# A decoder layer with 64 experts: a shorter choice of experts, and a part of the shared expert's products moved into the first pair

## The reference

```python
scores = sigmoid(h @ router_w)                   # 256 tokens x 64 experts
sel = scores + router_bias
group_score = sum of the two highest sel in each of 8 groups of 8 experts
emask = experts of the 4 best groups             # ties: the lower index
eidx = top 6 of where(emask, sel, -inf)
w = scores[eidx] / sum(scores[eidx]) * 2.5
routed = sum over the chosen experts of w * ((silu(h @ w1) * (h @ w3)) @ w2)
shared = (silu(h @ sw1) * (h @ sw3)) @ sw2       # one expert that sees all tokens
x = x + gate_f * (routed + shared);  out = rms_norm(x)
```

## Time and profile before

| | us |
|---|---|
| median of 3 runs | 773.07 (772.6 to 773.08) |
| the profiled execution | 774.05 |
| its span, first to last instruction | 772.3 |
| PE busy | 734.6 (95%) |
| DVE busy | 327.5 (42%) |
| ACT busy | 173.5 (22%) |
| DMA, mean over the span | 352 GB/s |

### The profile page before, as it was taken

How to read it: one execution, slowest core, us unless ns; L and a number is a source line. 1 busy time by engine, 2 the same in 40 slices (tenths; PEclk the granted TensorE clock), 3 DMA queues, 4 the chain that set the end, 5 groups by cost and what they waited for, 6 DMA issues and landing times.

```text
span 772.3 us, 12450 instructions
## 1 busy us (share of the span) xinstructions
PE 734.6 (95%) x5030; PEld 384.8 (50%) x5030; DVE 327.5 (42%) x812; ACT 173.5 (22%) x348; POOL 8.1 (1%) x21
## 2 busy tenths in 40 slices
PE   4899999999999999999999999999999998899995
PEld 1478888888887444334343333334334342333332
DVE  1107694764456576333334333231333332322334
ACT  3213330200000232212222222221212222212223
POOL 0200001000000000000000000000000000000000
PEclk9999999999999999999999999999999999999998
DMA  9999635886969578999999999999999999999991
GB/s 338 380 349 364 211 107 196 267 263 228 293 200 408 242 304 306 369 423 421 418 380 418 421 420 420 415 421 415 421 421 422 416 417 421 421 421 419 421 393 71
DMA packets 76165, 271.46 MB, mean 352 GB/s; under 512 B 4728, under 2 KB 33536, under 8 KB 53456
## 3 DMA queue, kind: packets, MB, share of 16 engines
q1 hardware_dynamic: 74544, 264.78, 87.8%
q0 software_dynamic: 1264, 5.79, 2.0%
q10 hardware_dynamic: 304, 0.13, 0.1%
HBM read 269.62 MB, written 1.05 MB: 350 GB/s over the span
## 4 chain that ended last, share of the span: by engine, by line
PE 73%; DMA 19%; SPq 3%; DVE 2%; ACT 1%; issue 1%; DVEq 0%; ACTq 0%
PE bank L1145 71%; DMA ring<-exp_w_dram 16%; DMA ring<-w_in_dram 3%; SPq L369 2%; PE bank L1516 1%; SPq L372 1%; DMA reg<-reg 1%; DVE h_hT L1136 0%; DVE bank L1099 0%; DVE reg L982 0%; PE bank L1234 0%; ACT L618 0%; ACT h_hT L643 0%; ACT reg L530 0%; DVE y_part L1103 0%
## 5 line engine op out<-in xcount | busy, mean ns | idle before, releaser
L1145 PE MATMUL bank<-ring,h_hT 128*32 128x512 f32 (+2 forms) x2112 | 262.4, 589 | 11.5 <-DMA ring<-exp_w_dram 11.5
L1145 PE MATMUL bank<-h_hT,ring 128*128 128x256 f32 x704 | 155.9, 380 | 2.5 <-DMA ring<-w_in_dram 2.5
L1145 PEld LDWEIGHTS bank<-ring,h_hT 128*32 128x32 f32 (+1 forms) x2112 | 80.6, 114 | 153.3 <-issue 133.3
L1145 PEld LDWEIGHTS bank<-h_hT,ring 128*128 128x128 f32 x704 | 133.2, 190 | 22.2 <-ACT h_hT L502 2.1
L1145 PE MATMUL bank<-ring,const_misc 128*32 128x512 f32 x1008 | 116.5, 595 | 0.7
L1099 DVE TENSOR_TENSOR bank<-bank,reg 128x512 f32<-128x512 f32 x64 | 44.5, 695 | 54.6 <-PE bank L1145 54.6
L1103 DVE TENSOR_TENSOR y_part<-bank,y_part 128x512 fp32r<-128x512 f32 x64 | 44.2, 691 | 42.5 <-ACT y_part L669 21.2
L1145 PEld LDWEIGHTS bank<-ring,const_misc 128*32 128x32 f32 x1008 | 30.2, 109 | 62.3 <-issue 57.6
L658 ACT ACTIVATE reg<-bank 128x256 f32<-128x256 f32 x32 | 12.3, 386 | 205.3 <-PE bank L1145 205.3
L1082 DVE TENSOR_TENSOR reg<-reg,bank 128x256 f32<-128x256 f32 x32 | 13.5, 421 | 102.2 <-ACT reg L658 102.2
L1145 PEld LDWEIGHTS bank<-take,h_part 128*128 128x128 f32 x288 | 38.8, 190 | 28.6 <-issue 27.6
(11 more groups left out here) (234 smaller groups left out, 459.1 us busy)
## 6 DMA issues: line engine op xcount, KB each, us to landing
ring<-exp_w_dram SPq DMA_DIRECT2D x171, 1024.0 KB, 14.8
ring<-ada_w_dram SPq DMA_DIRECT2D x24, 1024.0 KB, 12.7
ring<-w_in_dram SPq DMA_DIRECT2D x24, 1024.0 KB, 12.2
ring<-exp_w_dram SPq DMA_DIRECT2D x35, 512.0 KB, 13.5
ring<-w_branch_dram SPq DMA_DIRECT2D x4, 1024.0 KB, 12.8
ring<-w_out_dram SPq DMA_DIRECT2D x4, 1024.0 KB, 8.9
ring<-shared_w_dram SPq DMA_DIRECT2D x2, 1024.0 KB, 15.2
spare<-exp_w_dram SPq DMA_DIRECT2D x2, 1024.0 KB, 14.5
```

What stands on the lines that cost most here:

```text
L1145: return pe.matmul(o, lhsT, rhs, start=start, stop=stop, skip_group_check=True)
```

## The change

In `pick`, the count of the greater ones comes from the comparison itself (`accum_out`), the running count of the equal ones starts from it instead of zero, and the limit is the constant k; the comparisons take the k-th value as a scalar column. The add of the two marks is left to the caller: for the groups it goes into one step with the making of the mask, and the mask is multiplied by 1e30 where it is added to `sel`. In `place`, `iota` counts from 1, so that `pos` needs no subtraction, and the four comparisons are one of 256 columns. Both leave what is chosen as it was.

Of block 1's shared products, the steps k = 5, 6 and 7 (`SHARED_CUT`) move from before the gathers into the first pair, ahead of its first gather. Since the gathered tokens overwrite hT, ACT first copies these three slices to `hT_late`; DVE and PE wait for it (`hT_kept`). Block 1 uses bank 2 instead of 4. ACT's second shared sigmoid and DVE's `shared_product(1)` move into the first pair too, and one step of the others, k = 2, moves behind `rank(1)`. `cast_out(7)` moves ahead of DVE's first copy and uses bank 3, which the second first gather writes, so that this gather waits for it. The two first w2 transfers of half 1 are asked for behind the upper halves of pair 2's w1/w3, since `sh_done` comes later. The first body of ACT and DVE is written out instead of a loop.

```diff
             def load_pair(r, use, it, halves, first_e=0):
...
                     for e in range(first_e, 2):
                         for w in range(first_e if cols == HIGH else 0, 2):
                             load_13(r, e, w, it, cols)
+                if isinstance(use, int) and use == 1 and r == 0:
+                    first_load_2(1)
                 sp.wait_ge(w2_used[r], use)
...
             shared_sigmoid(0)
-            shared_sigmoid(1)
+            act.activation(hT_late[:, :, :], hT[:, SHARED_CUT:KD, P:2 * P], ACT.Copy).then_inc(S["hT_kept"], 1)
...
                     act.activation(give[:, r, :], bank[B_Y[0]][:, 0:P], ACT.Copy)\
                        .then_inc(S["give_read"], 1)
+                    if isinstance(use, int) and n == 0:
+                        shared_sigmoid(1)
                     copy_gathered(0)
...
                 link(dve.max(top8[:, tb, :], vals))
-                kth = top8[:, tb, k - 1:k].to_broadcast([P, n])
-                link(dve.tensor_tensor(m_gt, vals, kth, ALU.is_gt))
-                link(dve.tensor_tensor(m_eq, vals, kth, ALU.is_equal))
-                link(dve.tensor_reduce(need[:, tb:tb + 1], m_gt, AX, ALU.add))
-                link(dve.tensor_scalar(need[:, tb:tb + 1], need[:, tb:tb + 1], -1.0, float(k), ALU.mult, ALU.add))
-                link(dve.tensor_tensor_scan(m_pre, cn("ones", 0, n), m_eq, 0.0, ALU.mult, ALU.add))
-                link(dve.scalar_tensor_tensor(out=m_eq, in0=m_pre, scalar=need[:, tb:tb + 1], in1=m_eq,
-                                              op0=ALU.is_le, op1=ALU.mult))
-                return dve.tensor_tensor(m_gt, m_gt, m_eq, ALU.add)
+                kth = top8[:, tb, k - 1:k]
+                dve.tensor_scalar(m_gt, vals, kth, 0.0, ALU.is_gt, ALU.add, accum_out=need[:, tb:tb + 1])
+                link(dve.tensor_scalar(m_eq, vals, kth, None, ALU.is_equal))
+                link(dve.tensor_tensor_scan(m_pre, cn("ones", 0, n), m_eq, need[:, tb:tb + 1], ALU.mult, ALU.add))
+                link(dve.scalar_tensor_tensor(out=m_eq, in0=m_pre, scalar=float(k), in1=m_eq, op0=ALU.is_le, op1=ALU.mult))
...
-                link(dve.tensor_scalar(pos[:, tb, :], pos[:, tb, :], -1.0, None, ALU.add))
-                for m in range(GROUP):
-                    pp = pos[:, tb, 2 * m:2 * m + 2].unsqueeze(2).to_broadcast([P, 2, CAP])
-                    dve.tensor_tensor(take[:, 0, m, tb, :].rearrange("p (e s) -> p e s", e=2), iota, pp, ALU.is_equal)\
-                       .then_inc(S["take_built"], 1)
+                pp = pos[:, tb, 0:2 * GROUP].rearrange("p (m e) -> p m e", m=GROUP).unsqueeze(3).to_broadcast([P, GROUP, 2, CAP])
+                dve.tensor_tensor(take[:, 0, :, tb, :].rearrange("p m (e s) -> p m e s", e=2), iota_g, pp, ALU.is_equal)\
+                   .then_inc(S["take_built"], GROUP)
...
             passes_needed()
+            cast_out(7)
+            dve.wait_ge(S["hT_kept"], 1)
...
-            shared_product(1)
-            cast_out(7)
...
+                    if isinstance(use, int) and n == 0:
+                        shared_product(1)
                     dve.wait_ge(S["turn_done"], n + 1)
...
             shared_hidden(0, 4, KD)
             shared_hidden(1, 0, 1)
             rank(0)
-            shared_hidden(1, 1, 3)
+            shared_hidden(1, 1, 2)
             rank(1)
-            shared_hidden(1, 3, KD)
+            shared_hidden(1, 2, SHARED_CUT)
...
             def first_gather(k):
+                if k == 1:
+                    pe.wait_ge(S["cast_read"], 8)
...
                     if first:
-                        pe.wait_ge(S["sh_hid"], TB)
+                        pe.wait_ge(S["sh_hid"], 1)
+                        pe.wait_ge(S["hT_kept"], 1)
+                        shared_hidden(1, SHARED_CUT, KD)
                     gather(1 - parity, 2 * gm)
```

More of the change, by code:

```diff
@@ L65 @@
 FIRST_READS = 6
+SHARED_CUT = 5
 AHEAD = 2
@@ L244, in decoder_layer @@
         h_part = [sb(f"h_part{i}", [P, TB, KD, P], F32R) for i in range(2)]
+        hT_late = sb("hT_late", [P, KD - SHARED_CUT, P])
         hid_s = router[:, :, :].rearrange("p k e -> p (k e)").rearrange("p (t f) -> p t f", t=TB)
@@ L275, in decoder_layer @@
         B_UNIT_0 = [0, 4]
-        B_CAST = [3, 3, 3, 3, 3, 3, 3, 2]
+        B_CAST = 3
         B_OUT = [0, 1, 2, 3]
@@ L280, in decoder_layer @@
         B_SCORE = [0, 1]
-        B_SHARED = [7, 4]
+        B_SHARED = [7, 2]
         landed = [sem(f"landed{s}") for s in range(SLOTS)]
@@ L302, in decoder_layer @@
             take_built pair_gates gate_mm slot_gated gathered gath_read first_read sig1_done th_done hid_done turn_done turn_read
-            sw2_gated x2_top give_read y0_done y_gated y_top y_low y_high pos_next sum_done x3_sq x3_var x3_rstd fin_done stored""".split()
+            sw2_gated x2_top hT_kept give_read y0_done y_gated y_top y_low y_high pos_next sum_done x3_sq x3_var x3_rstd fin_done stored""".split()
         S = {n: sem(n) for n in names}
@@ L402, in load_body, with first_load_2 @@
                         load_pair(r, body * BODY_STEPS + j, of * BODY_STEPS + j, 2 * j + r == BODY_PAIRS - 1)
+            def first_load_2(r):
+                for e in range(2):
+                    sp.wait_ge(*used_up(LAST[6 * r + 4 + e]))
+                    load_2(r, e, 0)
             def load_spare_half(j):
@@ L421, in _ @@
                     load_spare_half(0)
-                for e in range(2):
-                    sp.wait_ge(*used_up(LAST[6 * r + 4 + e]))
-                    load_2(r, e, 0)
+                if r == 0:
+                    first_load_2(r)
             for step in range(1, BODY_STEPS):
@@ L671, in body @@
                     act.activation(y_part[0][:, 512:D], bank[B_Y[1]][:, :], ACT.Copy).then_inc(S["y_top"], 1)
-            with act.Fori(0, SPLIT) as use:
+            body(0)
+            with act.Fori(1, SPLIT) as use:
                 body(use)
@@ L900, in cast_out @@
                     dve.wait_ge(S["bias_in"], 80)
-                ins = dve.tensor_tensor(dst, bank[B_CAST[m]][:, :], dst, ALU.add)
+                ins = dve.tensor_tensor(dst, bank[B_CAST][:, :], dst, ALU.add)
                 if m // 2 == 1:
@@ L984, in route @@
                 link(dve.tensor_tensor(gs[:, tb, :], top[:, tb, :, 0], top[:, tb, :, 1], ALU.add))
[L985 to L992, removed]
+                pick(tb, gs[:, tb, :], GROUPS, TOPG, gt_g[:, tb, :], eq_g[:, tb, :], pre_g[:, tb, :])
+                link(dve.scalar_tensor_tensor(out=gt_g[:, tb, :], in0=eq_g[:, tb, :], scalar=-1.0, in1=gt_g[:, tb, :],
+                                              op0=ALU.add, op1=ALU.add))
+                link(dve.scalar_tensor_tensor(out=sel[:, tb, :].rearrange("p (g i) -> p g i", g=GROUPS),
+                                              in0=gt_g[:, tb, :].unsqueeze(2).to_broadcast([P, GROUPS, 8]), scalar=-NEG,
+                                              in1=sel[:, tb, :].rearrange("p (g i) -> p g i", g=GROUPS),
+                                              op0=ALU.mult, op1=ALU.add))
+                pick(tb, sel[:, tb, :], E, TOPK, picked[:, tb, :], eq[:, tb, :], pre[:, tb, :])
+                dve.tensor_tensor(picked[:, tb, :], picked[:, tb, :], eq[:, tb, :], ALU.add).then_inc(S["picked_done"], 1)
+            iota_g = cn("iota").unsqueeze(1).unsqueeze(1).to_broadcast([P, GROUP, 2, CAP])
             iota_2 = cn("iota").unsqueeze(1).unsqueeze(1).to_broadcast([P, TB, 2, CAP])
@@ L1104, in body @@
                            .then_inc(S["y_high" if hf else "y_low"], 1)
-            with dve.Fori(0, 1) as use:
-                body(use)
+            body(0)
             dve.wait_ge(S["cast_read"], 8)
@@ L1303, in cast @@
                 if m:
-                    pe.wait_ge(S["cast_read"], min(m, 6))
-                mm(bank[B_CAST[m]][:, :], cn("ones", 0, P), part2[:, m % 2, :]).then_inc(S["cast_done"], 1)
+                    pe.wait_ge(S["cast_read"], m)
+                mm(bank[B_CAST][:, :], cn("ones", 0, P), part2[:, m % 2, :]).then_inc(S["cast_done"], 1)
             def branch(g):
@@ L1398, in shared_hidden @@
                 for k in range(first, last):
-                    ins = mm(bank[B_SHARED[tb]][:, :].rearrange("p (w f) -> p w f", w=2), hT[:, k, tb * P:(tb + 1) * P],
+                    h_k = hT_late[:, k - SHARED_CUT, :] if tb and k >= SHARED_CUT else hT[:, k, tb * P:(tb + 1) * P]
+                    ins = mm(bank[B_SHARED[tb]][:, :].rearrange("p (w f) -> p w f", w=2), h_k,
                              sw13[:, :, k, :], k == 0, k == KD - 1)
@@ L1578, in constants @@
         c["inv"][64 * (g % 2):64 * (g % 2) + 64, (g // 2) * T:(g // 2 + 1) * T] = 1.0 / np.minimum(t, 2 ** (g + 1))
-    c["iota"][:] = np.arange(CAP)
+    c["iota"][:] = np.arange(CAP) + 1
     c["fold_f"][:] = i % 32 == np.arange(HEADS)
```

2 lines of the change are left out of this document (1 added, 1 removed).

## The result

Two comparisons of the changed kernel with the kernel before were made. The first gave medians of 775.47 and 773.07 us and a ratio of 1.0025 (95% interval 1.0016 to 1.0035), the second 774.50 and 773.07 and 1.0014 (1.0005 to 1.0022). Both intervals lie above 1. The change makes the kernel slower by 0.14 or 0.25%, 1.1 or 1.9 us. The prediction was +0.6 us, no change that can be told: the sign and the mechanism of 0.7 us are right, the rest of the loss, 0.4 to 1.2 us, is missing.

The account below looks back on a forecast made before the run. DMA was taken to bound the expert stage, the end standing a fixed distance behind TensorE's release at 388.60. First pair 1.6 us sooner, then 4.7 instead of 2.5 to its second products: +0.6, median 773.7 us, range 772.2 to 775.1.

Parts of the forecast that it names:

- rival 3: Expert pair 1: reordered w2 requests land after 323.6 and the pair waits; 2.0 us slower, 775.1; chance 0.07.
- the stated case: Whole kernel: second products start 0.6 us later and the end follows, 773.7, no change that can be told; chance 0.63.
- The choice: Expert choice on VectorE: 1.1 us less per block; block 1's ends at 287.3 instead of 289.34.
- First gather 2.1 sooner: Before the first pair: first gather starts at 291.85 instead of 293.98, held by VectorE alone.
- cast wait: Second first gather: waits for cast_out(7), the last cast, and starts at 293.03 instead of a possible 292.5; 0.5 us lost.
- first pair 1.6 sooner: First expert pair on TensorE: starts at 295.2 instead of 296.78.
- 4.7 from the end of the first products to the second: First pair on TensorE: moved shared products 2.6, gather and copy 1.4, then 0.7 us; 4.7 instead of 2.5.
- Start of the second products +0.6: First pair on TensorE: -1.6 + 4.7 - 2.5 makes second products start 0.6 us later, at 310.0.
- Requests: DMA stream: two w2 transfers asked for at 308.1 instead of 294.44, landed by 317.6; nothing reaches the end.
- Rival 2: TensorE's clock falls at new waits between 291 and 310, costing 1.7 us more: 775.4; chance 0.06.
- Rival 4: First pair: without both new waits of 0.5 us, the sum is -0.4, 772.7, counted as no change; chance 0.15.
- Rival 1: First pair: the release at 305.3 instead of 306.9 carries through to the end, 771.5; chance 0.09 with other gains over 0.2%.

Follow-up runs that it names:

- requests given back: Changed kernel, its three moved k steps reading pair 1's weights, so the first two w2 requests of half 1 go out early: 1.0009 to the kernel before, +0.7 us.
- late requests: Kernel before, with only the first two w2 requests of ring half 1 moved behind the upper halves of pair 2's w1/w3: 1.0048, +3.7 us.
- one moved step: Kernel before with shorter choice, only k = 7 moved behind the first pair's first gather, its weights copied aside, requests early, no cast wait: 0.9989, -0.85 us.

## Why the prediction was right and where it failed

- *The number*: 773.7 was forecast; by the two ratios it is 774.2 and 775.0. That both lie in the range of 772.2 to 775.1 is in part luck: the upper end was the price of rival 3, whose late w2 at pair 1 did not occur, and the stated case accounts for 0.7 us of 1.1 to 1.9.
- *The choice*: right. It ends 0.43 behind the mark instead of 2.44, two us sooner, TensorE's products hide that, and alone it is worth 0.5 (not clear of none).
- *First gather 2.1 sooner, cast wait, first pair 1.6 sooner, 4.7 from the end of the first products to the second*: from the mark 2.03, 0.44, 1.43 and 309.62 - 304.94 = 4.68. Right. TensorE's waits between 288 and 310 add up to 1.5 before and 2.1 after, not 1.8 and 2.3; the growth is about as forecast.
- *Start of the second products +0.6*: 0.73.
- *Requests*: here it failed. "The DMA stream idles 5 us more near 296 and less afterwards, and the next requests at 321.0 find it dry or nearly so, as now. Nothing of it reaches the end." The 5 us were right: the DMA share fell from 0.91 to 0.59 of 15 us, 4.8 us. "Less afterwards" was counted too high. The slack of the kernel before was 1.9 us at 320 (13 us at 359 instead of 421 GB/s) and 2.0 us at 388 (14 us at 360), less than the two transfers' 5 us together. The stream did not run dry at 321; it was 1 MB, 2.4 us, behind. The prediction then took over from the kernel before that TensorE has no wait for DMA up to the release at 388.60. In the changed kernel it waits at pair 6, and that release comes 1.47 late, not 0.7. That the end stands at a fixed distance behind this release held within 0.6 us (0.7 over all versions). With the requests given back, the changed kernel loses 0.7, which is the forecast; by difference the other 0.4 to 1.2 us are theirs. That late requests cost time by themselves is shown where nothing else was touched, in the kernel before (3.7 us) and in the one with one moved step (2.2 us); how much of the changed kernel's loss is theirs is known only within the overlapping intervals.
- *Rival 3* came nearest in name, but at the wrong place: it looked for late w2 at pair 1. TensorE has no wait for DMA there; what came late were the weights of pair 6, some 74 us behind the requests at 308.
- *Rival 2*: no fall of the clock near 300 (1.00 in every window there). It did come at pair 6 in the version with the late requests. A long wait alone does not bring it: the changed kernel waited 2.96 us at 645 and kept its clock, the kernel before fell behind 2.52 us.
- *Rival 4*: the waits of 0.5 were real and both could be removed, 0.71 and 0.68 us. That did not help the end as it assumed, because of the requests.
- *Rival 1*: the release at 305.07 lies 18.70 behind the mark; before, it was at 307.03, 20.13 behind it. The release was 1.43 earlier and did not carry through; the end came later.

## What to carry to other kernels

A step that is moved later takes along whatever waits for the buffers that it frees: here three moved k steps cost 0.7 us on TensorE's path, and the two transfers that could not be asked for before they were through some 0.4 to 1.2 us more, and 2.2 to 3.9 us where they were delayed by themselves. In a kernel that DMA bounds in the long run, keep a ledger of bytes asked for against time, at the rate that these transfers really have, before counting the compute path; a dry window is slack that can be used up, and waits that are absent from the trace of before can appear behind it. To fill a wait, put as much work into it as it is long, behind the instruction whose copy others need, and copy its operands aside so that the buffers stay free.

## What the runs showed of the hardware

- Transfers of 512 KiB, half the columns of a 1 MiB slot, moved 333 GB/s with the DMA engines 0.98 busy (late requests, 304 to 309); whole slots moved 405 at 1.02 (312 to 320). Why the halves are slower no run here shows.
- An instruction with a sum output on VectorE (0.28 us for 64 columns) is followed by a read of the accumulator of 0.08 us that overlaps the next operation.
- Behind a wait for DMA of 2.31 us a group of 32 products took 5.22 us instead of 3.64, at a granted clock of 0.88 in the window; behind one of 2.96 us in the changed kernel (the row below) it took 3.64, and in the kernel before, behind 2.52 us, 5.06. So the length of the wait alone does not decide it:
```profile
645.16 3.64 PE L1153 MATMUL bank<-ring,h_hT 128*32 128x512 f32 x32 [2.96 <-DMA ring<-exp_w_dram]
```
